# Two raw weight buffers in place of four in a streamed transformer block

## The reference

```
u = rmsnorm(h) * g                      # h = meta tokens, then frames
proj = u @ w_in                         # q, k, v, gate of 8 retention heads; cq, ckv, kr of the latent attention
ret_out = silu(rg) * head_groupnorm(retention_chunkwise(rq, rk, rv))
mla_out = rmsnorm(latent attention of (c_q @ w_uq, c_kv, k_rope, w_uk, w_uv))
h = h + concat(ret_out, mla_out) @ w_o
m = rmsnorm(h)
h = h + square(relu(m @ w_up)) @ w_down
return rmsnorm(h[frames])
```

## Time and profile before

| | |
|---|---|
| median of 3 runs | 1147.01 us (1146.83 to 1148.44) |
| the profiled execution: its time, its span | 1147.86 us, 1145.7 us |
| PE busy | 1124.1 us, 98% |
| DVE busy, ACT busy | 719.4 us (63%), 603.8 us (53%) |
| DMA | 206.63 MB, mean 180 GB/s |

### The profile page before, as it was taken

The page is one execution under the profiler, slowest core; times in us unless marked ns, Lnnn a source line. Parts: engine busy times, 40 slices in busy tenths (PEclk is TensorE's granted clock), DMA queues, the critical chain, the costliest instruction groups (busy, mean ns, idle before and its releaser), DMA issues.

```text
span 1145.7 us, 16770 instructions
## 1 busy us (share of the span) xinstructions
PE 1124.1 (98%) x6260; PEld 974.7 (85%) x6260; DVE 719.4 (63%) x964; ACT 603.8 (53%) x905; POOL 79.9 (7%) x82
## 2 busy tenths in 40 slices
PE   7999999999989999999999999999999999999997
PEld 6889999999978888888888888888888888888885
DVE  6976877777786666666664544545666665455453
ACT  8565666566655556555554333334555554344343
POOL 0001120211233330000000000000000000000000
PEclk9999999999989999999999999999999999999999
DMA  9544434444445655555555555555555555555541
GB/s 365 197 149 147 150 145 148 148 147 148 147 151 216 213 177 186 194 186 183 183 183 189 193 199 190 184 184 185 188 190 192 193 188 184 184 186 193 199 157 73
DMA packets 29572, 206.63 MB, mean 180 GB/s; under 512 B 3408, under 2 KB 3664, under 8 KB 5200
## 3 DMA queue, kind: packets, MB, share of 16 engines
q1 hardware_dynamic: 29232, 205.58, 50.2%
q10 hardware_dynamic: 288, 0.31, 0.1%
HBM read 203.79 MB, written 2.10 MB: 180 GB/s over the span
## 4 chain that ended last, share of the span: by engine, by line
PE 95%; DVE 2%; ACT 2%; DMA 1%; issue 0%; SPq 0%; DVEq 0%
PE acc L320 56%; PE ps_qn L320 10%; PE ps_qr L320 9%; PE ps_v L320 8%; PE ps_kn L320 8%; PE ps_x L320 2%; DMA x_in<-x_all 1%; DVE lo L982 1%; DVE x_sq L982 0%; ACT hi L677 0%; PE ps_y L320 0%; ACT x_sq L719 0%; ACT xs L715 0%; DVE mla_o L982 0%; PE ps_y L502 0%
## 5 line engine op out<-in xcount | busy, mean ns | idle before, releaser
L982 DVE TENSOR_TENSOR lo<-raw,hi 128x1024 fp32r<-128x1024 f32 (+1 forms) x379 | 463.6, 1224 | 292.4 <-ACT hi L677 288.2
L320 PE MATMUL acc<-xs,hi 128*128 128x512 f32 (+1 forms) x1952 | 586.1, 363 | 0.0
L677 ACT ACTIVATE hi<-raw 128x1024 fp32r<-128x1024 f32 (+1 forms) x379 | 398.5, 1052 | 299.1 <-PE ps_v L320 106.1
L320 PE MATMUL acc<-xs,lo 128*128 128x256 f32 (+1 forms) x1648 | 454.4, 284 | 9.5 <-DVE xs L999 6.7
L320 PEld LDWEIGHTS acc<-xs,hi 128*128 128x128 f32 x1952 | 344.8, 189 | 51.6
L320 PEld LDWEIGHTS acc<-xs,lo 128*128 128x128 f32 x1648 | 311.3, 189 | 17.1 <-issue 6.7
L677 ACT ACTIVATE half_b<-acc 128x256 f32<-128x256 f32 x100 | 38.6, 386 | 155.1 <-PE acc L320 155.1
L320 PE MATMUL ps_v<-hi,hid 128*128 128x512 f32 x256 | 101.4, 396 | 0.0
L320 PE MATMUL ps_kn<-hi,hid 128*128 128x512 f32 x256 | 100.7, 393 | 0.0
L320 PE MATMUL ps_qr<-hi,hid 128*128 128x512 f32 x256 | 100.3, 396 | 0.0
L320 PE MATMUL ps_qn<-hi,hid 128*128 128x512 f32 x256 | 99.6, 393 | 0.0
(11 more groups left out here) (242 smaller groups left out, 969.2 us busy)
## 6 DMA issues: line engine op xcount, KB each, us to landing
raw<-w_up SPq DMA_DIRECT2D x64, 1024.0 KB, 4.7
raw<-w_down SPq DMA_DIRECT2D x64, 1024.0 KB, 4.7
raw<-w_in SPq DMA_DIRECT2D x42, 1024.0 KB, 4.8
raw<-w_o SPq DMA_DIRECT2D x16, 1024.0 KB, 4.7
h_res<-x_frames SPq DMA_DIRECT2D x1, 2048.0 KB, 7.5
x_in<-x_all SPq DMA_DIRECT2D x3, 544.0 KB, 7.6
consts<-consts_in SPq DMA_DIRECT2D x1, 1217.5 KB, 10.2
raw<-w_in SPq DMA_DIRECT2D x2, 512.0 KB, 9.2
```

What stands on the lines that cost most here:

```text
L320: return pe.matmul(o, l, m, start=start, stop=stop)
L677: return act.activation(o, i, ACT.Copy)
L982: return dve.tensor_tensor(o, a, b, op)
```

## The change

RAWS becomes 2. A load of chunk c then waits for both lo halves of chunk c - 2 and not of chunk c - 4; raw, 8 KB per partition and buffer, shrinks from 32 KB to 16 KB, and what is placed behind it moves down. The count that ScalarE waits for in loops is adapted to the number of buffers. Orders of issue on all engines stay.

```
-RAWS = 4
+RAWS = 2
@@
                 if part == 0:
-                    act.wait_ge(raw_landed[c % RAWS], 16 * (c // RAWS + 1) + 4 * more)
+                    act.wait_ge(raw_landed[c % RAWS], 16 * (c // RAWS + 1) + 16 // RAWS * more)
```

## The result

The changed kernel takes 1158.93 us (median of 4 runs, 1158.72 to 1159.33) against 1147.55 us before on the same chips: ratio 1.0101, 95% interval 1.0086 to 1.0117, slower by 1%. The forecast was 1158.3.

What follows compares the result with a forecast made beforehand. TensorE, busy 1124.1 of 1145.7 us, was taken as the bound, so a loss must appear as a new wait. 2.4 + 6.9 + 2.0 = 11.3 us on 1147.0 gave 1158.3 us, range 1154.5 to 1163.

Steps and rivals of the forecast that it cites:

- The steady state is free: w_o and MLP chunks: loads with two buffers still land early enough; 170 and more of 188 chunks cost 0.
- 1.1 us is not the limit: Up stage: loads land 1.1 us before ScalarE needs them, but somewhat later would still cost TensorE nothing.
- The start, +2.4: First chunks: chunk 2's load waits for chunk 0's lo halves, putting ScalarE 2.4 us behind; bounds 1.5 and 3.4.
- The chain named: Start: ScalarE's squares of x and chunk 3's split, then VectorE's sum, delay TensorE's wait at 47.48 by 2.4 us.
- the one for consts: Start: consts lands at 35.8, TensorE waits 1.7 us for it, hidden under the start's 2.4 us.
- The end of attention, +6.9: Before turn(0): x_frames queues behind wo3's load, lands at 347.2, and TensorE waits 6.9 us (6.5 to 7.5).
- The clock, +2.0: After the 6.9 us wait TensorE's clock falls, costing 2.0 us, the middle of 1.4 and 2.5.
- Rival 1, the low clock twice: Start: its waits bring the clock down too, price 1.4 to 2.5 us, total 1160.3; chance 0.12.
- The sum, 11.3: Whole kernel: start 2.4, end of attention 6.9 and clock 2.0 make 11.3 us, giving 1158.3.

Runs made afterwards that it cites:

- 5.8 us later: Changed kernel, each MLP load waits for TensorE's first products of the second half of the chunk two ahead; 1167.71 us, ratio 1.0183.
- four buffers at the start: Changed kernel with chunks 2 and 3 given raw buffers of their own; 1157.32 us, ratio 1.0083 to the kernel before.
- x_frames before wo3: Changed kernel with x_frames issued ahead of the load of wo3; 1149.34 us, ratio 1.0017 to the kernel before.
- both undone: Changed kernel with both repairs: own buffers for chunks 2 and 3, x_frames ahead of wo3's load; 1146.99 us, ratio 0.9999.
- two buffers, repaired: Changed kernel, two buffers throughout, x_frames ahead of wo3's load, last retention head's sq_lo moved ahead on VectorE; 1146.95 us, ratio 0.9999.
- both undone, squares first: As both undone, with sq_lo of the last retention head ahead of wo1's split on VectorE; 1144.57 us, ratio 0.9978.
- copy of ckv first: Changed kernel, VectorE copies the first accumulator between chunk 2's two lo halves, not behind them; 1159.15 us, ratio 1.0108.
- 28 idle matmuls: Changed kernel with 28 matmuls on unused data ahead of turn(0) on TensorE; 1158.99 us, ratio 1.0103.
- MLP loads behind the next chunk's lo: Changed kernel, MLP loads wait for the first lo half of the chunk one ahead; 1346.25 us, ratio 1.1741.
- 8.6 us later loads: Changed kernel, each MLP load waits until TensorE is done with the chunk two ahead; 1304.05 us, ratio 1.1369.
- 32 idle matmuls: Changed kernel with 32 matmuls on unused data ahead of turn(0) on TensorE; 1158.22 us, ratio 1.0098.
- four buffers, the wait only: Kernel before, four buffers, plus one wait: x_frames issued only once VectorE has split wo1; 1154.74 us, ratio 1.0062.

## Why the prediction was right, point by point

- **The steady state is free**: right, shown by both repairs together (0.9999). That 1.1 us is not the limit is right too: 5.8 us later still left TensorE without a wait in steady stretches. The irregular places (the start of the MLP, the last two chunks) have less, which the prediction did not look at.
- **The start, +2.4**: right. It is 2.06 in the profile of the changed kernel. Over the nine profiles with two buffers at the start the M chunk begins at 65.5 to 66.4 (median 65.8), over the five with four there at 63.2 to 63.6 (median 63.4): 2.4 apart. By their ratios, three pairs of runs that differ only in the buffers of chunks 2 and 3 give 2.1 (the change against four buffers at the start), 2.1 (x_frames before wo3 against both undone) and 2.4 us (two buffers, repaired, against both undone, squares first). The chain named, ScalarE's squares, is enough to set it (copy of ckv first: no change). One step was wrong: TensorE was to start chunk 2 at 23.1, when its lo is ready. It started at 24.3, because it also waits for VectorE's copy of the accumulator, which stands behind both lo halves. The prediction asked what follows on ScalarE and not what is queued behind the late lo on VectorE. This wait hid the one for consts, which landed at 35.4 (35.8 was said) and showed as a wait only once the copy was moved.
- **The end of attention, +6.9**: right, 7.16. That it is the place in the queue is shown from both sides: moved forward, with two buffers, the wait is gone; held back, with four buffers, it appears. The parts of the 6.9 were off by more than their sum. x_frames was issued at 339.46 (339.8 was said), and the data was there 9.6 us after wo3's issue (10.0 was said, with 9.7 as the lower bound); from the landing to `turn(0)` it took 1.8 us (1.5 was said); and TensorE was there 0.7 us earlier, as the low clock behind the old wait was shorter. That these leave only 0.3 is luck.
- **The clock, +2.0**: right, 2.3 in the changed kernel's profile and 1.3 to 2.8 over five. That a wait of 3.62 us brings the clock down, on which the term rests, held in eleven of the twelve profiles that have this wait, and not in the one with 28 idle matmuls. After the waits of 5.5 us and more at `turn(0)` it was low in all seven. Wait and clock together were put at 8.9 us; the runs have 9.6 (1.0101 against 1.0017, and 1.0083 against 0.9999).
- **Rival 1, the low clock twice**: happened in part. In the changed kernel's profile the granted clock was 0.50 from 24.2 to 27.6, behind the wait of 2.33 us. It cost some 0.2 us and not the 1.4 to 2.5 that this rival was given: TensorE had time to spare before chunk 6. In the six profiles with two buffers at the start and the clock at 1.00 it waits there for 1.05 to 1.25 us. In the three with the low clock this wait is gone, and chunk 6 starts 0.35 us behind VectorE's result (49.31 and 49.67 in the changed kernel) and not 0.15. So there the two chains end nearly together, and TensorE's own is the last by a little.
- **The sum, 11.3**: the spans differ by 10.8 us and the medians by 11.4. In the profile of the changed kernel start, wait and clock are each off by 0.3, and TensorE's 0.7 us were not foreseen. That the medians are hit within 0.1 is luck as well.
- The Trainium skill (Trainium Kernel Development and Optimization, Best Practices) asks for double buffering to overlap DMA and compute. The steady state agrees, with TensorE busy for 200.00 of 200.00 us in the MLP. The cost came from elsewhere: 9.6 us from a transfer that shares the queue with the loads, and some 2 us from the first loads, which come before the steady state.

## What to carry to other kernels

When a ring of buffers is made shorter, look first at what else stands on the queue that fills it: a wait that is harmless for the next chunk holds back every other transfer behind it. The steady state tells little about the irregular places (first chunks, a tail of small operations, the last chunk), and there the price is paid. Put a transfer whose condition is met early ahead of a load whose condition is met late. And a wait that is moved later is only a delay as long as it does not close a loop with the chunk just before.

## What was not expected of the hardware

- Waits of TensorE of 2.33 to 2.53 us at the same place, 24.3 to 25.1 us, were followed by the low clock in three profiles (the change, the 5.8 us later loads, 28 idle matmuls) and not in five (x_frames before wo3, two buffers repaired, MLP loads behind the next chunk's lo, 8.6 us later loads, 32 idle matmuls). After waits of 5.5 us and more at `turn(0)` without the idle matmuls it was low each time. How long it stays low also varies behind the same wait of 3.62 us: it ends between 2.9 (four buffers, the wait only) and 5.9 us (ckv copy first) after the restart, at 5.4 in the earlier trace rows. In the profile with 28 idle matmuls, whose place in the program comes later, it did not fall there at all. TensorE's restart behind that wait, and the window from it on:

```profile
330.83 0.36 PE L320 MATMUL ps_y<-sq_lo,ones_r 128*128 128x256 f32 x1 [3.62 <-DVE sq_lo L984]
```

```profile
330.83:336.00 5.17, 5.17 (x30) 4.57 (x31) 3.90 (x6) 4.63 (x8) 0.69 (x2) 1.00 0.00 0
```

So one profile does not tell what the clock costs behind a wait of 2 to 4 us.

- x_frames behind a 1 MB load landed 9.1 to 9.3 us after its issue in six profiles (the change, and the five others in which TensorE stood idle for 6.4 us or more), and 10.4 and 10.5 us in the two in which TensorE ran idle matmuls meanwhile. Whether these slow the transfer was not tested.
